# A feed-forward down projection recast as seven block products over transferred token blocks

## The reference, cut to what matters

```python
D_MODEL = 1024
D_FF = -(-8 * D_MODEL // (3 * 256)) * 256      # 2816
h = rms_norm(x, norm_ffn_w[layer]) * (1.0 + sc_f) + sh_f
x = x + g_f * ((jax.nn.silu(h @ w_gate[layer]) * (h @ w_up[layer])) @ w_down[layer])
```

## Time and profile before

| what | us |
|---|---|
| time, median of 3 runs | 3846.37 (3841.93 to 3848.84) |
| the profiled execution's own time | 3848.22 |
| its span, first to last instruction | 3846.4 |
| PE busy / DVE / ACT / POOL | 3573.5 / 2123.2 / 1050.0 / 1417.0 |
| mean granted PE clock | 0.967 of full |

### The profile page before, as it was taken

One profiled execution on the slowest core, in us unless ns is written; L12 is line 12 of the kernel. 1 busy time (PEld: TensorE's weight loads), 2 busy tenths in 40 slices (PEclk: granted clock), 3 DMA queues, 4 the chain that ended last, 5 costly groups with the idle time before them and its releaser, 6 DMA issues. The chain is left out here.

```text
span 3846.4 us, 69485 instructions
## 1 busy us (share of the span) xinstructions
PE 3573.5 (93%) x29720; PEld 3369.0 (88%) x29720; DVE 2123.2 (55%) x3046; ACT 1050.0 (27%) x1728; POOL 1417.0 (37%) x1135
## 2 busy tenths in 40 slices
PE   7999978887989899999999999988869899999998
PEld 6999967776659899999999999977759899999998
DVE  5543655664874665555545544346665754555445
ACT  2000125552641243333100233024430433332100
POOL 5222221120003377777432322220003577776331
PEclk8999989998999999999999999989989999999999
DMA  6455531002331122222322233232241122223321
GB/s 215 163 179 174 176 105 32 22 22 67 78 97 42 29 68 74 71 73 69 124 91 60 64 111 117 88 102 84 72 122 46 41 73 74 70 74 100 102 85 72
DMA packets 393189, 339.26 MB, mean 88 GB/s; under 512 B 19683, under 2 KB 363233, under 8 KB 386766
## 3 DMA queue, kind: packets, MB, share of 16 engines
q1 hardware_dynamic: 381568, 290.89, 24.9%
q10 hardware_dynamic: 11214, 44.33, 2.9%
q0 software_dynamic: 128, 0.00, 0.2%
HBM read 249.95 MB, written 85.24 MB: 87 GB/s over the span
## 5 line engine op out<-in xcount | busy, mean ns | idle before, releaser
L1280 PE MATMUL ffn_acc<-ffn_BH,ffn_WH 128*128 128x384 f32 x1232 | 416.8, 338 | 25.3 <-DVE ffn_BL L1497 12.3
L1280 PE MATMUL ffn_acc<-ffn_BL,ffn_WH 128*128 128x384 f32 x1232 | 416.1, 338 | 0.0
L1280 PE MATMUL ffn_acc<-ffn_BH,ffn_WL 128*128 128x384 f32 x1232 | 415.5, 337 | 0.0
L1217 POOL TENSOR_TENSOR ffn_WL<-raw,ffn_WH 128x512 fp32r<-128x512 f32 x176 | 296.1, 1684 | 266.1 <-ACT ffn_WH L1366 266.1
L1707 PE MATMUL ffn_acc<-ffn_BH,ffn_WH 128*128 128x384 f32 x1056 | 354.3, 336 | 8.7 <-DVE ffn_S L1786 4.3
L1707 PE MATMUL ffn_acc<-ffn_BL,ffn_WH 128*128 128x384 f32 x1056 | 353.8, 335 | 0.0
L641 PE MATMUL in_ab_acc<-hH,in_ab_wH 128*128 128x384 f32 (+2 forms) x840 | 288.9, 344 | 7.0 <-DVE hL L502 6.9
L641 PE MATMUL in_ab_acc<-hL,in_ab_wH 128*128 128x384 f32 (+2 forms) x840 | 285.3, 340 | 0.0
L1217 POOL TENSOR_TENSOR ffn_WL<-ffn_S,ffn_WH 128x512 fp32r<-128x512 f32 x176 | 272.1, 1555 | 18.5 <-ACT ffn_WH L1366 18.3
L641 PE MATMUL in_c_acc<-hH,in_c_wH 128*128 128x384 f32 (+1 forms) x768 | 261.4, 340 | 6.8 <-DVE hL L502 6.8
L641 PE MATMUL in_c_acc<-hL,in_c_wH 128*128 128x384 f32 (+1 forms) x768 | 261.3, 340 | 0.0
(11 more groups left out here) (624 smaller groups left out, 8236.8 us busy)
## 6 DMA issues: line engine op xcount, KB each, us to landing
in_ab_ada<-in_ada_w SPq DMA_DIRECT2D x40, 1024.0 KB, 5.0
hidden<-ffn_up SPq DMA_DIRECT2D x44, 576.0 KB, 2.8
raw<-in_w_gate SPq DMA_DIRECT2D x44, 512.0 KB, 3.8
raw<-in_w_up SPq DMA_DIRECT2D x44, 512.0 KB
raw<-in_w_down SPq DMA_DIRECT2D x80, 256.0 KB, 2.7
pT<-in_ab_out ACTq DMA_DIRECT2D x34, 576.0 KB, 3.3
pT<-in_c_out ACTq DMA_DIRECT2D x32, 576.0 KB, 3.7
raw<-in_w_in_ab SPq DMA_DIRECT2D x34, 512.0 KB, 4.5
```

The costliest lines, as they stand in the source:

```text
L1217: self.nc.gpsimd.tensor_tensor(self.WL[:, slot], src, self.WH[:, slot].bitcast(F32), ALU.subtract).then_inc(lo, 1)
L1280: ins = self.nc.tensor.matmul(self.acc[:, bank, 0:n], w[:, slot, k, :], x(low, k), start=start and k == 0 and w is self.WH and low == 0, s ...
```

## The change

The way down is now done by the same class as the ways up. The hidden tiles are taken in pairs (q = 0 to 10), the even tile as the first half of the inner dimension and the odd one as the second. Three parts of 4, 4 and 3 pairs, each with 4 groups of two output tiles, give 12 more groups after the 22, numbered 22 to 33. A group of a part with h pairs has 11 products of 3h matmuls.

The nine token blocks of a part are not made from chunks on the chip any more but stored by the ways up: for each pair DVE forms four differences (`multiply`), and SP stores nine blocks of [128, 384] to `hidden`, now `[9, 11, 128, 384]`. The even tile is kept in the room of `sumsq`, which is therefore cleared later. When a part begins, each of its nine blocks ([128, h, 384], 768 KB for h = 4) is loaded as a whole into the place of the rests (`BL` or `hL`) as soon as the last product that uses the old block is done (`load_block`), rounded by ACT into `BH`/`hH` in h operations (`round_block`) and subtracted in place by DVE in h operations (`low_block`). In `pe_group` the third chunk moved behind P1 and P2, and its halves changed places: P1, P2, far half 1, far half 0, P5, P6, P3, far, P7, P4, far.

What it does to the order, on three engines around the first refill:

The diff, cut to its core:

```diff
...
-        far(2, BFAR1, 0, True).then_inc(self.far1a_mm, 1)
-        pe.wait_ge(self.u3_copied, j)
-        mixed(2, BX, B11, stop=False).then_inc(self.p1_mm, 1)
-        pe.wait_ge(self.a12_lo, j + 1)
-        far(3, BFAR1, 1, False).then_inc(self.far1_mm, 1)
-        pe.wait_ge(self.c21_done, j)
-        mixed(3, BY, B21).then_inc(self.p2_mm, 1)
+        far(3, BFAR1, 1, True, n=n, h=h, before=fresh(FAR_1)).then_inc(self.far1b_mm, 1)
+        far(2, BFAR1, 0, False, n=n, h=h, before=fresh(FAR_0)).then_inc(self.far1_mm, 1)
         pe.wait_ge(self.s1_lo, j + 1)
         pe.wait_ge(self.c22_done, j)
-        mixed(0, BZ, T1).then_inc(self.p5_mm, 1)
+        mixed(0, BZ, T1, h=h, before=fresh(T1)).then_inc(self.p5_mm, 1)
...
+    def last_low(self, dve, j):
+        h = self.halves[j]
+        if h < HALF:
+            dve.wait_ge(self.a21_hi, j + 1)
+            self.nc.vector.tensor_tensor(self.WL[:, 1, 0:h], self.A21[j], self.WH[:, 1, 0:h].bitcast(F32), ALU.subtract
+                                         ).then_inc(self.a21_lo, 1)
...
-    parts = (2, 4, 4, 4, 4, 4)
-    N = KF
-    first_k = [sum(parts[:p]) for p in range(len(parts))]
-    part_with = [p for p, n in enumerate(parts) for _ in range(n)]
-    n_down = KD * len(parts)
...
+    parts = (4, 4, 3)
+    first_q = [sum(parts[:p]) for p in range(len(parts))]
+    PAIRS_OUT = KD // 2
+    n_down = PAIRS_OUT * len(parts)
+    halves = [HALF] * N + [parts[i // PAIRS_OUT] for i in range(n_down)]
+    G = N + n_down
...
+            def load_block(p, name):
+                if name == B11:
+                    qs = first_q[p] + parts[p]
+                    sp.wait_ge(m.t_lo, 8)
+                    sp.wait_ge(even_stored, 48 * qs)
+                    sp.wait_ge(odd_stored, 48 * qs)
+                    sp.wait_ge(mixed_stored, 48 * qs)
+                sp.wait_ge(last_use[name], N + p * PAIRS_OUT)
+                h = parts[p]
+                sp.dma_start(rooms_of(name, h)[1].bitcast(F32), g.hidden[name, first_q[p]:first_q[p] + h].rearrange("q p c -> p q c")
+                             ).then_inc(u_in[FRESH.index(name)], 16)
+
+            load2(0)
+            for j in range(G):
+                p = before_part(j)
+                if p is not None:
+                    load_block(p, B11)
+                    load_block(p, B21)
+                load1(j + 1)
+                if p is not None:
+                    load_block(p, T1)
+                    load_block(p, T2)
+                    load_block(p, B22)
+                    load_block(p, FAR_1)
+                    load_block(p, T3)
+                load2(j + 1)
+                if p is not None:
+                    load_block(p, T4)
+                    load_block(p, FAR_0)
+                if j < N:
+                    store(j)
...
         def _(act):
...
+            def free1(act, j):
+                if j <= N:
+                    act.wait_ge(hidden_done, j)
                 else:
-                    act.wait_ge(down_mm, KD * (p - 1))
-                act.wait_ge(u_in[k % 2], 16 * (k // 2 + 1))
-                nc.scalar.copy(hidden_part(m.BH, p)[:, k - first_k[p], :], stage_of(k)).then_inc(u_hi, 1)
+                    act.wait_ge(m.near1, j)
+
+            def round_block(p, name):
+                h = parts[p]
+                hi, room = rooms_of(name, h)
+                act.wait_ge(u_in[FRESH.index(name)], 16 * (p + 1))
+                for i in range(h):
+                    nc.scalar.copy(hi[:, i, :], room[:, i, :].bitcast(F32)).then_inc(u_hi, 1)
+
+            def refill(j, place):
+                p, last = before_part(j), before_part(j - 1)
+                if last is not None and place == 0:
+                    round_block(last, FAR_0)
+                    round_block(last, B22)
+                if last is not None and place == 1:
+                    round_block(last, T3)
+                if last is not None and place == 2:
+                    round_block(last, T4)
+                if p is not None and place == 1:
+                    round_block(p, B11)
+                if p is not None and place == 2:
+                    round_block(p, B21)
...
         def _(dve):
...
                 dve.wait_ge(silu_done, j + 1)
                 dve.wait_ge(m.near2, j + 1)
                 dve.wait_ge(m.far2_out, j + 1)
-                stt(up[:, 0:TP], up[:, 0:TP], bias[:, 1, 0:1], gated[:, 0:TP], ALU.add, ALU.mult)
+                if not odd and q:
+                    dve.wait_ge(mixed_stored, 48 * q)
+                stt(out[:, 0:TP], up[:, 0:TP], bias[:, 1, 0:1], gated[:, 0:TP], ALU.add, ALU.mult)
                 dve.wait_ge(m.far2_added, j + 1)
-                tt(up[:, TP:T], up[:, TP:T], gated[:, TP:T], ALU.mult).then_inc(hidden_done, 1)
-
-            def low_hidden(k):
-                p = part_with[k]
-                at = k - first_k[p]
-                dve.wait_ge(u_hi, k + 1)
-                tt(hidden_part(m.BL, p)[:, at, :], stage_of(k), hidden_part(m.BH, p)[:, at, :].bitcast(F32), ALU.subtract
-                   ).then_inc(u_lo, 1)
-
-            def add_tile(i):
-                p, n = part_of(i)
-                u, last = i % 2, p == len(parts) - 1
-                pair, third = down_banks[u]
-                dve.wait_ge(down_mm, i + 1)
-                xs = g.xT[:, n, 0:two].rearrange("p (c n) -> p c n", n=CH)
-                stt(xs, acc[:, pair:pair + 2, 0:CH], gate[:, n, 0:1], xs, ALU.mult, ALU.add)
-                stt(g.xT[:, n, two:TP], acc[:, third, 0:TP - two], gate[:, n, 0:1], g.xT[:, n, two:TP], ALU.mult, ALU.add)
+                tt(out[:, TP:T], up[:, TP:T], gated[:, TP:T], ALU.mult).then_inc(hidden_done, 1)
+                dve.wait_ge(hidden_done, j + 1)
+                if odd:
+                    dve.wait_ge(even_stored, 48 * (q + 1))
+                    tt(even[:, chunk(1)], up[:, chunk(1)], even[:, chunk(1)], ALU.subtract).then_inc(t_done, 1)
+                    tt(extra, up[:, chunk(1)], extra, ALU.subtract).then_inc(t_done, 1)
+                    dve.wait_ge(t_done, 4 * q + 3)
+                    tt(even[:, chunk(0)], up[:, chunk(0)], extra, ALU.subtract).then_inc(t_done, 1)
+                else:
+                    tt(extra, even[:, chunk(1)], even[:, chunk(0)], ALU.subtract).then_inc(t_done, 1)
...
+            def low_block(p, name):
+                h = parts[p]
+                hi, room = rooms_of(name, h)
+                for i in range(h):
+                    dve.wait_ge(u_hi, first_unit(p, name) + i + 1)
+                    tt(room[:, i, :], room[:, i, :].bitcast(F32), hi[:, i, :].bitcast(F32), ALU.subtract).then_inc(u_lo, 1)
...
+            def square(j, n):
+                at = 2 * part_of(j)[1] + n
+                if part_of(j)[0] == len(parts) - 1 and at < KD - 1:
+                    dve.wait_ge(added, 2 * (j - N) + n + 1)
+                    dve.wait_ge((m.near1, m.near2)[n], j + 1)
+                    if at:
+                        dve.wait_ge(sum_done, at)
+                    tt(sq, g.xT[:, at, :], g.xT[:, at, :], ALU.mult).then_inc(squared, 1)
+                    dve.wait_ge(squared, at + 1)
                     tt(g.sumsq[:, :], g.sumsq[:, :], sq, ALU.add).then_inc(sum_done, 1)
...
+                if last is not None:
+                    low_block(last, FAR_0)
+                m.take_far(dve, j, 0) if j < N else add_far(j, 0)
+                if last is not None:
+                    low_block(last, B22)
+                if p is not None:
+                    low_block(p, B11)
+                m.add_c12(dve, j, (lambda: low_block(last, T3)) if last is not None else (lambda: None))
+                m.last_low(dve, j)
+                if last is not None:
+                    low_block(last, T4)
+                if p is not None:
+                    low_block(p, B21)
+                    low_block(p, T1)
+                m.weigh1(dve, j) if j < N else add_near(j, 0)
+                if p is not None:
+                    low_block(p, T2)
                 m.take2(dve, j)
-                m.take_far(dve, j, 1)
-                multiply(j)
-            low_hidden(1)
-            for i in range(n_down):
-                p, n = part_of(i)
-                add_tile(i)
-                if p + 1 < len(parts) and n % 2 == 0:
-                    low_hidden(first_k[p + 1] + n // 2)
+                if p is not None:
+                    low_block(p, FAR_1)
+                m.weigh2(dve, j) if j < N else add_near(j, 1)
+                m.take_far(dve, j, 1) if j < N else add_far(j, 1)
+                if j < N:
+                    multiply(j)
+                if j == N:
+                    dve.wait_ge(mixed_stored, 48 * NQ)
+                    nc.vector.memset(g.sumsq[:, :], 0.0)
+                if j >= N:
+                    square(j, 0)
+                    square(j, 1)
...
```

390 lines of the change are left out of this document (197 added, 193 removed).

## The result

| | us, median (range) | ratio to before |
|---|---|---|
| kernel before | 3845.89 (3841.93 to 3848.84) | |
| changed kernel | 3882.09 (3881.18 to 3889.22) | 1.0099, 95% interval 1.0081 to 1.0116 |

The change makes the kernel 36 us slower; 3877 was forecast, in a range of 3816 to 3904. The profiled execution took 3881.37 us, its span is 3879.7, against 3848.22 and 3846.4 before: 33.3 us of span to account for.

A forecast was written before the change was run, and what follows sets the result against it. PE's matmuls were taken to set the pace, at 0.1736 us each. 87.4 us come and 56.1 go, net +31 on the profiled 3848.22 us: 3879, as a median 3877, range 3816 to 3904.

The forecast's parts named there:

- matmuls, old waits, clock: gone: Way down: 132 fewer matmuls save 22.9 us a layer, two DVE waits 4.3, half-rate clock 1.7 once; 56.1 in all.
- group 1: Group 1 of each layer: P2, now second product, waits 2.0 us for group 0's bank; +1.5 us a layer.
- refills: Groups 21, 22, 25, 26, 29, 30: loading, rounding and subtracting new blocks doesn't fit under PE; 12, 9 and 4, together 25 us a layer.
- squares: Groups 31 to 33: DVE's squares, alternating with POOL, delay P3 by 4.6 us each; +13.8 us a layer.
- end of a way down: After PE's last matmul: DVE's third chunk and one square with its sum take 3.9 us, before 2.0; +1.9 a layer.
- clock: Half-rate clock after PE's new waits of up to 10 us: 1.5 us a layer, bounds 0 to 5.
- the steady groups: Groups up and down without new waits: the new order costs nothing; down with h = 4 takes 22.9 us, PE-bound.
- Turns: DVE and POOL operations reading two SBUF operands each wait out the other's whole operation; 19.5 of 23.2 us in a group up.
- Rival 1: DVE and POOL alternating does not bind: refills cost 10.4 us a layer, squares 0; -28 us, 3818; chance 0.21.
- rival 2: Only squares or only refills bind, not both: net about 0, 3847; chance 0.19.
- the walk of DVE: First refill, groups 21 and 22: DVE's operations timed in sequence; far half 0's first piece at 41.3 us, its product due at 31.
- rival 3: Refill transfers are the bound, 1536-byte rows at 253 GB/s: refills 37 us a layer, +24 more, 3901; chance 0.15.

## Why the prediction was right, step by step

| term, us, both layers | forecast | measured |
|---|---|---|
| matmuls, old waits, clock: gone | 56.1 | 56.2 (27.2 and 29.0) |
| group 1 | 3.0 | 5.3 |
| refills | 50 | 59.0, with their clock |
| squares | 27.6 | 20.9 |
| end of a way down | 3.8 | 3.5 |
| clock | 3.0 | within the above, some 8 |
| sum of what comes | 87.4 | 88.7 |

88.7 less 56.2 is 32.5 us, the spans show 33.3. The mechanism was the one forecast, but that the sums are so near is in part luck: the squares were charged 6.7 us too much, and group 1, the refills and the clock together 8.3 us too little.

**What goes and the steady groups** hold: 132 matmuls fewer, groups of 22.95 and 23.2 us without a wait.

**Turns** were the reason given, and the two kernels with one SBUF operand show them, each in its own groups: 20.9 us of squares to 0, 15.5 us off the refills. Rival 1 (turns don't bind, 3818) and rival 2 (one of the two binds) fall with them. What did not hold is the other side of the claim, that refills without turns would cost 20.8 us: without the turns of the rests they still cost 43.5, and only with small transfers as well 18.8. The Trainium skill ("SBUF — State Buffer", Who interferes with whom) has the rule that a DVE instruction with two SBUF inputs and a GpSimd one that reads SBUF exclude each other for a whole instruction. The runs agree: the four rests of far half 0 took 1.95 us with a second operand in PSUM and 4.04 with it in SBUF.

**Squares** were mis-sized: 4.6 us in each of three groups was forecast, 3.2 measured in those at full clock. The difference s4 came when it was forecast (10.5 us into the group), but its rest was charged one more turn, 3.4 us in place of 2.0; DVE had done its last square by then. (The sum of DVE's work in such a group, 8.4 us, should be 7.9 by its own terms, and 13.9 less 9.4 is 4.5; neither changes the argument.)

**Refills.** First 12 forecast, 14.9 and 13.8 measured; second 9, 9.1 in both; third 4, 6.6 and 5.6. In the first the walk of DVE was right within 1.5 us at the point that ends the wait. What it missed lies on both sides of it: groups 21 grew by 2.2 and 1.6 us, since PE stood 2.1 and 1.5 us at P1, where 1.6 was told but counted into one sum with the later wait; and behind the wait some 15 matmuls ran at half clock, which cost 2.2 us. The second came out by luck. The walk had P2 wait 1.8 us and the product with far half 1 end 4.0 us late; neither waits at all, since the rests of far half 1 ran beside a POOL that stood for its weights and were done 26.8 us after the start of group 25, not 32.7. The first rest of far half 0 began at 32.9 and not at 38.3. Its four pieces in 4.04 us and matmuls at half clock then brought the end of that product to 39.1, where the walk had 40.4. The third refill got no walk, only a guess by its smaller pieces, and that is where it was poorest.

**Transfers** (rival 3, 3901) are not the bound: cutting them to a quarter brought 7 us. But the forecast charged them and the turns as if one of them could be taken by itself. Without turns 15.5 us go, without transfers 4.6, without both 40.2: each covers the other, and neither experiment alone measures its cause.

**Clock.** This term was mis-sized: 3.0 us for both layers, some 8 by the rows. Group 1 and group 31 show the clock undiluted, since the same group with the same waits took 1.5 us more in the layer with the lower clock (27.66 and 26.12; 22.01 and 20.45), 3.1 us in all. In the refills PE kept busy gave back 3.6 and 1.7 us, 5.3. These 8.4 us sit in the table's other rows. The term's working, from one stretch after waits of 2 us, says nothing of groups that wait for 10.

**Group 1.** 1.5 forecast, 1.9 at full clock. The wait at P2 was 2.56 and not 2.0, since the addition that frees its bank ran at 1367.02 behind a weighing in turns with POOL (2.02 us); besides PE waited 0.66 us ahead of P1 for ACT's copy, in place of 0.47.

## What to carry to other kernels

A cut in matmuls is worth what it saves only if the engines that feed the operands can refill them between two uses; count for each refill the operations that read two SBUF operands on DVE and on GpSimd together, by the number of operations as well as by their columns, and place them before choosing the product order. When two causes delay the same chain, take both away in one run before giving either a price. And where a wait has moved to another product, look at what stands behind whom on the engine that feeds it: reading the next wait twice turned a version level with the kernel before into one 0.3% under it, and each time the edit was one of order. Last, compare a sum term by term: here two misses of 7 and 8 us stood against each other.

## What was not expected of the hardware

Fewer bytes made DVE slower: with transfers of 192 KB in place of 768, the four rests of far half 1 went from 2.13 to 5.40 us, because POOL was no longer waiting for its weights beside them (those of far half 0 behind them fell from 4.04 to 2.56).

A mean granted clock overstates what the clock costs where PE waits: group 22, at 0.86 over 35.6 us, misses 5.1 us of clock, of which 2.4 fall on matmuls. Even of that a part costs nothing where the operands come one piece at a time: the product with far half 0 in group 26 took 4.60 us at half clock and 4.26 at full.

After the same wait of 2.21 us on POOL the clock fell in group 31 of the first layer and not in group 32, which is 1.5 us shorter for it; no run here tells why.
